# Row sums of the gathered experts in sets of four groups, with nineteen row slots

## The reference

```python
def one(args):
    xb, ib, gb = args                      # 128 tokens, their 8 x 16 experts, their gates
    act = jax.nn.gelu(jnp.einsum("thkd,td->thk", u_tab[ib], xb)) * gb
    return jnp.einsum("thk,thkd->td", act, v_tab[ib])
```

## Time and profile before

| | |
|---|---|
| median of three runs | 2721.94 us |
| profiled execution | 2722.57 us |
| its span on the core | 2720.8 us |
| mean granted TensorE clock | 0.985 of full speed |
| TensorE busy with matmuls | 2633.9 us, 97% |
| VectorE, ScalarE, GpSimd busy | 61%, 38%, 26% |
| DMA moved | 704.65 MB, 259 GB/s over the span |

### The profile page before, as it was taken

The page is one execution under the profiler, slowest core; times in us unless marked ns, Lnnn a source line. Parts: engine busy times, 40 slices in busy tenths (PEclk is TensorE's granted clock), DMA queues, the critical chain, the costliest instruction groups (busy, mean ns, idle before and its releaser), DMA issues. The chain is left out here.

```text
span 2720.8 us, 39632 instructions
## 1 busy us (share of the span) xinstructions
PE 2633.9 (97%) x15897; PEld 2314.1 (85%) x15897; DVE 1653.3 (61%) x3299; ACT 1036.3 (38%) x1558; POOL 714.9 (26%) x676
## 2 busy tenths in 40 slices
PE   7998799999999999999999888999999999999998
PEld 6997699999999997777769778999999999777775
DVE  3437687878444456555566568987844445655556
ACT  3444433345433333333343564334543333333332
POOL 1001100000111116777733002000011111677773
PEclk9998999999999999999999899999999999999999
DMA  9643476356699869999962123335669986999994
GB/s 303 209 145 135 164 262 231 144 201 265 249 366 321 312 219 390 378 381 377 380 243 100 73 95 105 132 128 202 268 252 364 321 311 220 397 375 389 386 379 187
DMA packets 233109, 704.65 MB, mean 259 GB/s; under 512 B 22112, under 2 KB 154592, under 8 KB 211168
## 3 DMA queue, kind: packets, MB, share of 16 engines
q1 hardware_dynamic: 172912, 516.86, 51.7%
q0 software_dynamic: 59200, 184.79, 18.5%
q10 hardware_dynamic: 816, 0.48, 0.1%
HBM read 598.12 MB, written 103.94 MB: 258 GB/s over the span
## 5 line engine op out<-in xcount | busy, mean ns | idle before, releaser
L1359 PE MATMUL hidden_ps<-h_hi,u_hi 128*128 128x384 f32 x2016 | 680.1, 337 | 2.5 <-issue 1.5
L1359 PE MATMUL hidden_ps<-h_hi,u_lo 128*128 128x384 f32 x2016 | 674.0, 334 | 0.0
L1359 PE MATMUL hidden_ps<-h_lo,u_hi 128*128 128x384 f32 x2016 | 674.0, 334 | 0.0
L2262 DVE TENSOR_TENSOR v_lo<-v_slot,v_hi 128x1024 fp32r<-128x1024 f32 x248 | 304.9, 1229 | 305.4 <-ACT v_hi L2127 305.3
L2127 ACT ACTIVATE v_hi<-v_slot 128x1024 fp32r<-128x1024 f32 x248 | 262.9, 1060 | 532.8 <-PE out_ps L2058 532.8
L2058 PE MATMUL out_ps<-v_hi,act_hi 128*128 128x512 f32 x992 | 394.2, 397 | 0.6 <-DVE act_lo L2272 0.6
L2058 PE MATMUL out_ps<-v_lo,act_hi 128*128 128x512 f32 x992 | 387.7, 391 | 0.0
L2058 PE MATMUL out_ps<-v_hi,act_lo 128*128 128x512 f32 x992 | 386.3, 389 | 0.0
L1359 PEld LDWEIGHTS hidden_ps<-h_hi,u_hi 128*128 128x128 f32 x2016 | 378.7, 188 | 4.7 <-issue 4.7
L1359 PEld LDWEIGHTS hidden_ps<-h_lo,u_hi 128*128 128x128 f32 x2016 | 378.7, 188 | 0.0
L1359 PEld LDWEIGHTS hidden_ps<-h_hi,u_lo 128*128 128x128 f32 x2016 | 378.5, 188 | 0.0
(11 more groups left out here) (502 smaller groups left out, 4006.2 us busy)
## 6 DMA issues: line engine op xcount, KB each, us to landing
u_slot<-in_peer_u SPq DMA_DIRECT2D x64, 2048.0 KB, 9.1
v_slot<-in_peer_v SPq DMA_DIRECT2D x64, 2048.0 KB, 9.7
hidden<-hidden_ring SPq DMA_DIRECT2D x64, 768.0 KB, 5.9
spread_gates<-spread SPq DMA_DIRECT2D x16, 2048.0 KB, 8.1
hidden_in<-hidden SPq DMA_DIRECT2D x64, 512.0 KB, 14.3
ada_w_ring<-in_ada_w SPq DMA_DIRECT2D x48, 512.0 KB, 5.7
even_w_ring<-in_even_w SPq DMA_DIRECT2D x16, 1024.0 KB, 6.8
ada_w_ring<-in_ada_w SPq DMA_DIRECT2D x16, 1024.0 KB, 6.1
```

Source lines behind the costliest of these rows:

```text
L1359: mm = pe.matmul(PH_[:, b, 0:T], u[:, b, k * P:(k + 1) * P], x[:, k, :], start=(k == 0 and part == 0), stop=(k == KB - 1 and part == 2))
L2262: dve.tensor_tensor(lo, V[o // JC % 2][:, o % JC, :], hi.bitcast(F32), ALU.subtract).then_inc(vl, 1)
```

## The change

The 32 row sums now stand in 8 sets of four groups, after keys 20, 34, 48 and so on to 118 (`SET_AFTER`). The column products of a set stand together on VectorE, one key further ahead than before. The ring has 19 slots: eight new ones lie in the two slots of `u`, which are free by then. As the buffers of the late keys lie there too, ScalarE waits for all row sums before key 124. The rows of a group share one of six semaphores.

GpSimd's list becomes: rows 0 and 1, picks(0) and picks(1), rows 2 to 18, picks(2) to picks(6). Then for each set `s` it has 16 rows (each waits for the sum that frees its slot) and four groups of picks, 4s+7 to 4s+10. The picks have eight semaphores instead of four.

```diff
                 SLOT_AT = (M.picks, M.phase + 63488, M.u + 36864, M.u + 40960, M.u + 45056, *(20480 + 4096 * n for n in range(4)),
-                           M.phase, M.phase + 20480)
+                           M.phase, M.phase + 20480, *(M.u + 4096 * n for n in range(8)))
...
-                slot_in = [sem(st, f"row_in{n}") for n in range(RING)]
-                pick_in = [sem(st, f"picked_in{n}") for n in range(4)]
+                slot_in = [sem(st, f"row_in{n}") for n in range(6)]
+                pick_in = [sem(st, f"picked_in{n}") for n in range(8)]
...
-                QUAD_AFTER = [15 + i * (LATE - 17) // (QUADS - 1) for i in range(QUADS)]
+                SET = 4
+                SET_AFTER = [20 + 14 * i for i in range(8)]
...
-                    def row_sums(i):
-                        pe.wait_ge(acts_made, i + 1)
-                        for j in range(4 * i, 4 * i + 4):
-                            pe.wait_ge(slot_in[j % RING], 16 * (j // RING + 1))
-                        for c in range(2):
-                            for g in range(4):
-                                mm = pe.matmul(PO[TG * g:TG * g + TG, 0, c, :], SDW[:, i % 4, g, 31 - i:63 - i],
-                                               ROWS[(4 * i + g) % RING][:, c * CH:(c + 1) * CH],
-                                               start=(i == 0), stop=(i == QUADS - 1), skip_group_check=True)
-                        mm.then_inc(rows_summed, 1)
+                    def row_sums(s):
+                        groups = range(SET * s, SET * s + SET)
+                        pe.wait_ge(acts_made, SET * s + SET)
+                        for i in groups:
+                            pe.wait_ge(slot_in[i % 6], 64 * (i // 6 + 1))
+                            for c in range(2):
+                                for g in range(4):
+                                    mm = pe.matmul(PO[TG * g:TG * g + TG, 0, c, :], SDW[:, i % 4, g, 31 - i:63 - i],
+                                                   ROWS[(4 * i + g) % RING][:, c * CH:(c + 1) * CH],
+                                                   start=(i == 0), stop=(i == QUADS - 1), skip_group_check=True)
+                            mm.then_inc(rows_summed, 1)
...
-                        if o in QUAD_AFTER:
-                            row_sums(QUAD_AFTER.index(o))
+                        if o in SET_AFTER:
+                            row_sums(SET_AFTER.index(o))
...
                         if 3 <= o < LATE:
                             act.wait_ge(o_done, o - 2)
+                        if o == LATE:
+                            act.wait_ge(rows_summed, QUADS)
...
-                                                bass.IndirectOffsetOnAxis(ap=IDXV[:, t:t + 1], axis=0)).then_inc(slot_in[j % RING], 16)
+                                                bass.IndirectOffsetOnAxis(ap=IDXV[:, t:t + 1], axis=0)).then_inc(slot_in[j // 4 % 6], 16)
...
                     def picks(i):
-                        if i >= 4:
-                            pool.wait_ge(acts_made, i - 3)
+                        if i >= 8:
+                            pool.wait_ge(acts_made, i - 7)
...
                     for j in range(FREE, RING):
                         row(j)
-                    picks(2)
-                    at = RING
-                    for i in range(QUADS):
-                        while at < min(P, RING + 4 * i + 4):
-                            row(at)
-                            at += 1
-                        if i + 3 < QUADS:
-                            picks(i + 3)
+                    for i in range(2, 7):
+                        picks(i)
+                    for s in range(len(SET_AFTER)):
+                        for j in range(RING + 16 * s, min(P, RING + 16 * s + 16)):
+                            row(j)
+                        for i in range(SET * s + 7, min(QUADS, SET * s + 11)):
+                            picks(i)
...
                     def act_columns(i):
-                        dve.wait_ge(pick_in[i % 4], 64 * (i // 4 + 1))
+                        dve.wait_ge(pick_in[i % 8], 64 * (i // 8 + 1))
...
-                        if o + 1 in QUAD_AFTER:
-                            act_columns(QUAD_AFTER.index(o + 1))
+                        if o + 2 in SET_AFTER:
+                            for i in range(SET):
+                                act_columns(SET * SET_AFTER.index(o + 2) + i)
```

More of the change, by code:

```diff
@@ L1976, in peer_experts @@
                 QUADS = P // 4
-                QUAD_AFTER = [15 + i * (LATE - 17) // (QUADS - 1) for i in range(QUADS)]
+                SET = 4
+                SET_AFTER = [20 + 14 * i for i in range(8)]
                 EARLY_AFTER = {EARLY + 2 + 7 * e // 2: e for e in range(FIRST_U)}
-                assert QUAD_AFTER[-1] < LATE and max(EARLY_AFTER) < N_KEYS - 6
+                assert SET_AFTER[-1] < LATE and len(SET_AFTER) * SET == QUADS and max(EARLY_AFTER) < N_KEYS - 6
                 def token(i, g):
@@ L2183, in picks @@
                             pool.indirect_dma_start(ACT0[:, t:t + 1], None, hidden,
-                                                    bass.IndirectOffsetOnAxis(ap=IDXG[:, t:t + 1], axis=0)).then_inc(pick_in[i % 4], 16)
+                                                    bass.IndirectOffsetOnAxis(ap=IDXG[:, t:t + 1], axis=0)).then_inc(pick_in[i % 8], 16)
                     def early_load(e):
```

## The result

The changed kernel took 2815.51 us (median of six runs, 2810.80 to 2821.41) against 2720.88 us for the kernel before (six runs). The ratio is 1.0351, with a 95% interval of 1.0338 to 1.0364: 3.5% slower, some 95 us. The forecast was 2796 us, with a range of 2708 to 2840. The profiled execution took 2818.7 us, its span was 2816.9 us.

What follows compares the result with a forecast made beforehand. TensorE was taken to bound the kernel (busy 97%), with the DMA engines also at their limit in the output stretch. 2722.6 - 15.4 (sets) + 63 (late picks) + 26 (first set) = 2796 us, range 2708 to 2840.

Steps and rivals of the forecast that it cites:

- TensorE's gain: Layer output stretches: four row sums in a row pay the narrow-shape switch once, 7.25 us a set; -15.4 us for both layers.
- The first set: Start of each layer's sums: picks(2) and (3) queue behind 17 rows and come late, 13 us a layer, +26 us.
- Late picks at the later sets: Seven later sets a layer: picks behind 16 rows in GpSimd's queue come 4.5 us late each, +63 us (0 to 112).
- VectorE waits for `first_act` before the sets: Sign of being right: column products wait for DMA first_act, some 5 us before each of seven sets, more before the first.
- the 38.5 us from a set's start: Time after a set's start by which the next set's picks must land, or TensorE feels the delay.
- the two cases that the prediction had counted: Picks at a later set are 2.6 us late, or 8.0 if the third pair's v load (5.4 us) takes turns too.
- The middle value: Delay of picks taken for each later set: 4.5 us, near the middle of 2.6 and 8.0.
- rival C: v and hidden values late instead of picks, in stretches without sums: 35 us more, 2768 us; chance 0.15.
- Rival A: Before the column products: all picks in time, only TensorE's saving left, 2707 us or up to 2717; chance 0.20.
- Rival B: Only the first set of each layer late, later sets find their picks in time: 2733 us; chance 0.15.
- The DMA engines have no slack over a period: Per 14 keys and a set, 17.6 MB at 384 to 393 GB/s take 44.7 to 45.8 us of 45.3.
- turns between the queues: DMA engines serve queues in turn, a packet each, so v loads delay urgent picks; a period's delay nearer 8 than 2.6 us.

Runs made afterwards that it cites:

- short rows: Changed kernel, fetching 1 KB of each row and using it four times: 2717.63 us, ratio 0.9987; on a chip with ScalarE's standstill 3154.19 us, 1.1414.
- kernel with pairs: Changed kernel with sets of two groups every seven keys, eight rows first, requests in turn: 2712.51 us, ratio 0.9972; with ScalarE's standstill 2822.40 us, 1.0207.
- the run with the start only: Changed kernel with only picks(2) and picks(3) moved ahead of rows 2 to 18: 3161.34 us, ratio 1.1444, run only on a chip with ScalarE's standstill.

## Why the prediction was right, point by point

The direction and the mechanism held: 2796 us was forecast, 2815.5 measured, inside 2708 to 2840. That the sum came so near is in part luck, since a term that was too high stands against two that were missing, and the range is wide: it held a small gain as well. Its terms, for both layers together:

- **TensorE's gain, -15.4 us.** Right. A set takes 7.00 us to the next key and 7.22 with the edges (45.3 - 14 x 2.72, from the chain with short rows); 7.25 was forecast. The kernel with short rows agrees with the whole term within its interval.
- **The first set, +26 us.** TensorE waited 14.8 us in layer 0 and 14.7 in layer 1 for the picks behind 17 rows, 29.6 us. With a quarter of the row bytes 6.2 us a layer are left (5 was the lower bound, for empty queues), and the other three quarters cost the rest. How much would be left with no row bytes at all wasn't measured.
- **Late picks at the later sets, +63 us.** The mechanism was right: VectorE waits for `first_act` before the sets, as was named ahead, and the picks' place in the queue makes it. The size was too high. The later sets' waits of TensorE sum to 33.6 us (0.9 to 5.9 each, nine of fourteen), 2.4 us a set where 4.5 was taken. In layer 1 long and short waits take turns, and they go with the number of `v` loads in the 38.5 us from a set's start. After the set at 2416.96 three go out (the third at 2448.40), and the last pick lands after 18.75 us; after the set at 2470.99 it is two (the third follows at 2509.66), and it lands after 13.94. Those are the two cases that the prediction had counted, 5.4 us apart for the third load; the landing times differ by 4.8. No run tested that load by itself. The middle value that was taken holds for neither kind of set. Why the waits end before the last sets wasn't followed up.
- **Two terms were missing, which the sum had at nothing.** TensorE's waits for hidden values are 86.1 - 29.6 - 33.6 = 22.9 us. The forecast had them as rival C at 35 us, in place of the late picks; both came at once. And the granted clock fell behind the standstills. The six pieces x24 in layer 1's chain are 42.9 us long, against 6 x 5.68 = 34.1 at the full clock, 8.8 us in that layer. The remainder is 95 + 15.4 - 86.1 = 24 us for the clock and what else there is, in both layers.

So 63 was 29 too high, 26 was 4 too low, and 23 and 24 were left out. The sum was 20 us too low. Its own lower end doesn't follow from its terms: 1.5 us a set with 26 us at the start is 2754 us, not 2745.

- **Rival A** (all in time) was wrong by its own point: the picks weren't there at 38.5 us. With the row bytes cut it becomes true from the second set on.
- **Rival B** (only the first set) is refuted by nine later waits.
- **Rival C** (hidden values late) came true beside the forecast, at 23 us instead of 35.
- "The DMA engines have no slack over a period" was too strong. The kernel with pairs moves 397 GB/s over 300 us where the kernel before moved 385, and its periods are shorter (22.83 us for seven keys, 23.3 before). A period's 17.6 MB would be 44.3 us at that, a slack of 1 us.
- The landing times that the prediction took as bearing out turns between the queues are weak support: the median of 14.5 us for hidden values is itself from a stretch full of rows. The kernel with short rows gives the contrast. There hidden values land after 9.6 us at the median in layer 1's stretch. That shows that row bytes delay them, not in which order an engine serves its queues.

## What to carry to other kernels

Where two kinds of requests share a queue, what counts for the urgent one is what stands ahead of it in the queue, not how many groups ahead it is asked for. "Seven ahead" put the last group behind its own batch of rows; "eight ahead", with two groups ahead of the rows at the start, gave back 68 us. A grouping that saves 15 us on the engine that sets the time also turns a steady transfer into bursts. What won here, by 7.6 us, was to do it in small groups (pairs) and keep the requests in turn; how much each of the two brings wasn't separated. Count the first group separately, since it can be late even with few bytes. A standstill of TensorE can cost more than its length, as the clock comes back late (8.8 us over six of them in layer 1).

## What the runs showed of the hardware

- DMA share didn't show what was left: at a share of 1.01 the engines carried 385 GB/s over 300 us, and in the kernel with pairs 397 GB/s at 1.03.
- Behind a standstill of 14.7 us in layer 1 TensorE's first matmuls start 0.42 to 0.43 us apart instead of 0.23. The granted clock was 0.83 over the 40 us around it, and 0.50 in the standstill of 14.8 us in layer 0.
- The last pick that a set needed landed 18.75 us after its issue behind sixteen rows of 512 KB in the same queue, and 7.3 us after behind rows of 128 KB at the first set.
- On two of the chips ScalarE stood still for up to 25.6 us at a time (the run with the start only) while GpSimd issued long runs of requests. The same kernel that took 1.0102 of the kernel before elsewhere took 1.1416 there. A ranking of such kernels from one chip doesn't hold for all.
